# First block of a fused kernel: weight remainders one step later, gates by tanh, modulation through landing halves, bias remainder on VectorE

## The reference, cut to what matters

```python
mod = silu(c) @ w_ada + b_ada             # 1024 x 6144: twelve slabs of 512 columns, ada0 to ada11
h, hc = norm(x) * (1 + sc) + sh, norm(ctx) * (1 + sc_c) + sh_c      # slabs 0 to 3
na_k, na_v, ml_k, ml_v, ml_g, na_q, ml_q, ml_o, gate_na, gate_ml = split(h @ w_in)   # ctx: the first five
o_na = neighbourhood_attention(...)       # 8 heads of 64, 256 queries, 256 + 256 keys
o_ml = mlstm(...)                         # 4 heads, both directions
merged = sigmoid(gate_na) * (o_na @ w_branch_na) + sigmoid(gate_ml) * (o_ml @ w_branch_ml)
x = x + gt_m * rmsnorm(merged @ w_out, g_mix_post)
x = x + gt_f * rmsnorm(moe_ffn(...))      # 32 experts, 12.6 MB of weights each
x = second_block(x)                       # two layers
```

## Time and profile before

| | |
|---|---|
| median of 3 runs | 2408.9 us (2406.7 to 2418.7) |
| the profiled execution | 2409.3 us, its span 2407.5 us |
| first block up to the first expert matmul | 0 to 440 us of the span |
| experts | 440 to some 1360 us |
| second block | to 2407.5 us |
| TensorE busy, mean granted clock | 91%, 0.971 |

### The profile page before, as it was taken

How to read it: one execution, slowest core, us unless ns; L and a number is a source line. 1 busy time by engine, 2 the same in 40 slices (tenths; PEclk the granted TensorE clock), 3 DMA queues, 4 the chain that set the end, 5 groups by cost and what they waited for, 6 DMA issues and landing times.

```text
span 2407.5 us, 33072 instructions
## 1 busy us (share of the span) xinstructions
PE 2201.5 (91%) x13860; PEld 1569.3 (65%) x13860; DVE 929.6 (39%) x1355; ACT 734.7 (31%) x969; POOL 28.1 (1%) x32
## 2 busy tenths in 40 slices
PE   5999888999889888988998899999999799999998
PEld 4887676433333333333333488998999698998997
DVE  4456575311111121111121265366344454474453
ACT  4124552211101111111111245444433444544432
POOL 0000011000000000000000000000000000000000
PEclk8999998999999999999999999999999899999998
DMA  9462156699999999999999934544444454443542
GB/s 359 165 225 90 53 158 212 255 428 427 427 427 428 428 427 428 427 428 428 426 428 428 358 113 159 160 163 153 145 162 167 141 168 148 147 170 137 178 154 92
DMA packets 139388, 626.98 MB, mean 260 GB/s; under 512 B 7703, under 2 KB 33831, under 8 KB 114407
## 3 DMA queue, kind: packets, MB, share of 16 engines
q1 hardware_dynamic: 131808, 609.87, 65.0%
q0 software_dynamic: 5184, 13.90, 2.0%
q10 hardware_dynamic: 2247, 1.01, 0.2%
HBM read 623.69 MB, written 1.05 MB: 259 GB/s over the span
## 4 chain that ended last, share of the span: by engine, by line
PE 65%; DMA 23%; DVE 5%; issue 3%; ACT 3%; SPq 1%; ACTq 0%; DVEq 0%; POOL 0%
DMA ring<-in_w_lin 20%; PE bank L1598 15%; PE bank L1687 12%; PE bank L1922 10%; PE bank L1937 5%; PE bank L1845 3%; DMA ring<-in_w_in 2%; PE bank L1268 2%; PE bank L1316 2%; PE bank L1864 1%; DVE ring_rounded L2027 1%; PE bank L1711 1%; PE bank L1253 1%; PE bank L1696 1%; PE bank L1465 1%
## 5 line engine op out<-in xcount | busy, mean ns | idle before, releaser
L1598 PE MATMUL bank<-ring,arenaA 128*64 128x512 f32 x3072 | 692.9, 601 | 39.3 <-DMA ring<-in_w_lin 28.6
L1598 PEld LDWEIGHTS bank<-ring,arenaA 128*64 128x64 f32 x3072 | 211.0, 138 | 462.1 <-issue 390.3
L2475 DVE TENSOR_TENSOR ring_rounded<-ring,ring_rounded 128x2048 fp32r<-128x2048 f32 (+1 forms) x160 | 338.1, 2152 | 148.1 <-ACT ring_rounded L964 148.1
L964 ACT ACTIVATE ring_rounded<-ring 128x2048 fp32r<-128x2048 f32 (+1 forms) x160 | 280.4, 1799 | 284.7 <-DMA ring<-in_w_in 116.2
L1687 PE MATMUL bank<-arena_rounded,ring_rounded 128*128 128x256 f32 x2496 | 308.9, 284 | 0.0
L1687 PEld LDWEIGHTS bank<-arena_rounded,ring_rounded 128*128 128x128 f32 x2496 | 301.1, 190 | 4.1 <-issue 3.1
L1922 PE MATMUL bank<-arena_rounded,ring_rounded 128*128 128x256 f32 x2112 | 256.0, 282 | 1.2 <-DVE arena_rounded L2665 1.0
L1922 PEld LDWEIGHTS bank<-arena_rounded,ring_rounded 128*128 128x128 f32 x2112 | 252.8, 190 | 4.6 <-ACT arena_rounded L1106 3.0
L2421 DVE TENSOR_SCALAR arenaA<-bank 128x512 f32<-128x512 f32 x32 | 22.1, 692 | 502.4 <-PE bank L1598 502.4
L945 ACT ACTIVATE arenaA<-bank 128x512 f32<-128x512 f32 x32 | 19.1, 597 | 328.8 <-PE bank L1643 328.8
L1937 PE MATMUL bank<-arena_rounded,ring_rounded 128*128 128x256 f32 x912 | 110.0, 283 | 2.3 <-DVE arenaA L2677 2.3
(11 more groups left out here) (385 smaller groups left out, 2210.6 us busy)
## 6 DMA issues: line engine op xcount, KB each, us to landing
ring<-in_w_gate SPq DMA_DIRECT2D x64, 2048.0 KB, 23.3
ring<-in_w_lin SPq DMA_DIRECT2D x64, 2048.0 KB, 25.6
ring<-in_w_down SPq DMA_DIRECT2D x64, 2048.0 KB, 21.8
ring<-in_w_in SPq DMA_DIRECT2D x34, 2048.0 KB, 12.0
ring<-in_w_ffn_gate SPq DMA_DIRECT2D x10, 2048.0 KB, 8.1
ring<-in_w_ffn_up SPq DMA_DIRECT2D x10, 2048.0 KB, 7.8
ring<-in_w_ffn_down SPq DMA_DIRECT2D x12, 1536.0 KB, 6.4
ring<-in_w_in SPq DMA_DIRECT2D x16, 1024.0 KB, 8.0
```

The source lines that it names most:

```text
L964: act.activation(place2(name + "_hi", ringR)[:, a:b, :], place2(name)[:, a:b, :], ACT.Copy).then_inc(w_hi, 1)
L1598: last = pe.matmul(bank[b][k * SLOTS:(k + 1) * SLOTS, :], lhsT(c), slot(j)[:, c % 4, k * 512:(k + 1) * 512], start=False, stop=(c == DC - ...
L2475: dve.tensor_tensor(place2(name, ringR)[:, a:b, :], w[:, a:b, :], hi[:, a:b, :], ALU.subtract).then_inc(w_lo, 1)
```

## The change

- nak0 and nak1 become one 2 MB slab nak, with its high part in place 5; the rounding has two pieces, each ahead of one of the copies of ada rows 2 and 3.
- ada10 and ada11 leave the ring. All slabs 4 to 11 come through the landing buffers; each buffer has a semaphore and is refilled as soon as its own four steps are done. The folds 4 to 11 all stand in the projections, and so do VectorE's steps for them. The load of the gate columns (mlgRaw) is issued behind ada4 on GpSimd's queue.
- The ring is filled up with two empty slabs, so expert 0's first loads go to places 4, 5 and then 0 to 3.
- Attention: ScalarE rounds gate h+2 in the even step, VectorE forms its remainder in the odd one; bna0 and bna1 follow in the last two heads; the later remainders move up by one.
- Gates: tanh(x/2) in place of sigmoid(x); the branch product is multiplied by (1 + gate), which doubles merged; scale 0.5 in the output's squares and in gpost takes it out.
- out1 is rounded right behind the square root of the head norm.
- The bias remainder is formed by VectorE behind out3's remainder; ScalarE's copy for it moves behind the rounding of out3.
- Eight identity matmuls on TensorE behind the turns of ada2 and ada3.

```diff
-        adaRow = [Pna[:, 1, :] if i < 4 else wide(AT_MLO, 2, 512, arenaA)[:, i % 2, :] if i < 10 else cossin[:, :]
-                  for i in range(12)]
+        adaRow = [Pna[:, 1, :] if i < 4 else wide(AT_MLO, 2, 512, arenaA)[:, i % 2, :] for i in range(12)]
...
-        slabs += [(f"nak{i}", half(C_NAK + 256 * i)) for i in range(2)]
-        slabs += [("nav", w_in[:, :, C_NAV:C_MLK]), ("nav_hi", None),
+        slabs += [("nak", w_in[:, :, C_NAK:C_NAV]), ("nak_hi", None), ("nav", w_in[:, :, C_NAV:C_MLK]), ("nav_hi", None),
...
-        for k in range(8):
-            slabs += [(f"gate{k}", half(gate_at[k]))]
-            if k in (0, 2):
-                slabs += [(f"ada{10 + k // 2}", ada_src(10 + k // 2))]
+        slabs += [(f"gate{k}", half(gate_at[k])) for k in range(8)]
...
+        slabs += [(None, None)] * (-len(slabs) % RING)
...
+        ORDER1 = [f"na_k{m}" for m in range(4)] + ["na_v0", "na_v1", "ada4", "na_v2", "ada5", "na_v3", "ml_k0", "ada6", "ml_k1", "ada7",
+                                                  "ml_v0", "ml_v1", "ml_v2", "ada8", "ml_v3", "ada9", "ml_g", "ml_q0", "ml_gt", "ada10",
+                                                  "na_q0", "ada11", "na_q1", "ml_o0", "ml_o1"]
...
-            for j in range(RING):
+            for j in (4, 5, 0, 1, 2, 3):
                 sp.wait_ge(*freed(N1 - RING + j))
                 expert_slab(0, j)
...
-            rounded1("nak0")
+            rounded1("nak", (0,))
             ada_copy(2)
-            rounded1("nak1")
+            rounded1("nak", (1,))
             ada_copy(3)
...
-                    empty(GATES[h], dst, ACT.Sigmoid, src=two)
-                    if h + 2 < 8:
-                        rounded1(f"gate{h + 2}")
-                    elif h == 7:
-                        rounded1("bna0")
+                    empty(GATES[h], dst, ACT.Tanh, scale=0.5, src=two)
+                elif h + 2 < 8:
+                    rounded1(f"gate{h + 2}")
+                elif h == 6:
+                    rounded1("bna0")
+                else:
+                    rounded1("bna1")
...
-                if dr == 1:
-                    rounded1(("bna1", "bml0", "bml1", "out0")[h])
+                if dr == 1 and h < 3:
+                    rounded1(("bml0", "bml1", "out0")[h])
...
             rounded1("out2")
             rounded1("out3")
+            act.wait_ge(bias_in, 16 * 6)
+            act.activation(bparts, braw, ACT.Copy).then_inc(bias_hi, 1)
             act.wait_ge(c_pos, 1)
...
+            for _ in range(8):
+                pe.matmul(bank[4][:, 0:P], K["ident"][:, :], K["ident"][:, :], start=True, stop=True)
...
-                pe.wait_ge(ada_sum, i - 3)
+                pe.wait_ge(ada_sum, 2 * (i - 3))
...
-                if i in (8, 14):
-                    ada_fold(9 + i // 7)
...
-                if i < 10:
-                    dve.wait_ge(ada_in, 32 * (i - 3))
-                    w = lambda c: adaX[c // 4][:, c % 4, :]
-                else:
-                    dve.wait_ge(*in1(f"ada{i}"))
-                    w = lambda c: raw1(f"ada{i}")[:, c, :]
+                w = lambda c: adaX[c // 4][:, c % 4, :]
                 for c in chunks:
+                    if c % 4 == 0:
+                        dve.wait_ge(ada_in[c // 4], 16 * (i - 3))
...
             rest1("nav")
             ada_part(4, range(8))
+            ada_part(5, range(4))
             rel_copy(0)
-            ada_part(5, range(4))
+            ada_part(5, range(4, 8))
+            rest1("mlk")
             rel_copy(1)
-            ada_part(5, range(4, 8))
+            modulation(4)
+            ada_part(6, range(8))
             rel_copy(2)
...
             rest1("naq0")
             rest1("naq1")
-            modulation(6)
-            ada_part(8, range(8))
-            modulation(7)
+            modulation(8)
+            ada_part(10, range(8))
+            modulation(9)
+            ada_part(11, range(4))
...
-                if qt and h + 2 < 8:
-                    rest1(f"gate{h + 2}")
+                if qt:
+                    rest1(f"gate{h + 2}" if h + 2 < 8 else f"bna{h - 6}")
...
-            rest1("bna0")
...
-                link(dve.tensor_tensor(gm, bank[g % 4][:, :].rearrange("p (a b) -> p a b", a=2), gm, ALU.mult))
+                link(dve.scalar_tensor_tensor(out=gm, in0=gm, scalar=1.0, in1=two(bank[g % 4][:, :]), op0=ALU.add, op1=ALU.mult))
...
             rest1("out2")
             rest1("out3")
+            dve.wait_ge(bias_hi, 1)
+            for k in range(2):
+                r = slice(64 * k + 32, 64 * k + 64)
+                dve.tensor_tensor(bparts[r, :, :], braw[r, :, :], bparts[r, :, :].bitcast(F32), ALU.subtract).then_inc(bias_lo, 1)
...
-            pool.dma_start(mlgRaw, w_in[:, :, C_MLG:C_NAQ]).then_inc(bg_in, 16)
-            for i in range(4, 10):
-                pool.wait_ge(*((lin_done, G1["ada3"] + 1) if i == 4 else (ada_sum, i - 4)))
+            pool.wait_ge(lin_done, G1["ada3"] + 1)
+            for i in range(4, 12):
                 for k in range(2):
-                    pool.dma_start(adaX[k], ada_src(i)[:, 4 * k:4 * k + 4, :]).then_inc(ada_in, 16)
+                    if i > 4:
+                        pool.wait_ge(ada_sum, 2 * (i - 5) + k + 1)
+                    pool.dma_start(adaX[k], ada_src(i)[:, 4 * k:4 * k + 4, :]).then_inc(ada_in[k], 16)
+                if i == 4:
+                    pool.dma_start(mlgRaw, w_in[:, :, C_MLG:C_NAQ]).then_inc(bg_in, 16)
...
-            pool.wait_ge(bias_hi, 1)
-            for k in range(2):
-                r = slice(64 * k + 32, 64 * k + 64)
-                pool.tensor_tensor(bparts[r, :, :], braw[r, :, :], bparts[r, :, :].bitcast(F32), ALU.subtract).then_inc(bias_lo, 1)
```

107 lines of the change are left out of this document (48 added, 59 removed).

## The result

The changed kernel takes 2391.5 us (median of 4 runs, 2388.2 to 2396.2), the kernel before 2408.9; the ratio is 0.9928, with a 95% interval of 0.9903 to 0.9954, 17.4 us between the medians. The forecast was 2392.3 us and -17.0.

A forecast was written before the change was run, and what follows sets the result against it. TensorE and what it waits for bound the first 440 us; the experts' weight stream behind, at 427 GB/s, only moves with it. Terms summed to -17.0 us, from 2409.3 to 2392.3 us; range 2384 to 2402.

The forecast's parts named there:

- Attention, -17.8: Attention stage: without late loads and waits TensorE alone sets the pace, 11.15 us a pair; 17.8 us shorter, bounds -14 and -18.3.
- Projections: folds +1.9: Projections: the two folds moved here from the attention take 0.95 us each, adding 1.9 us.
- Fold 11, +1.1: End of projections: fold 11 waits 3.2 us where fold 9 waited 2.09, adding 1.1 us; bounds -1.3 and +5.2.
- No further half-speed groups: Projections: no more groups of 24 matmuls than before take 7.38 instead of 5.83 us at the dropped clock.
- Rival 1: Projections: folds behind more short rel matmuls bring three more clock drops, +4.7 us, 2397 us; chance 0.14.
- Start, +1.7: Start: both roundings and row copies come behind the whole nak slab's landing, adding 1.7 us; bounds +0.4 and +2.4.
- mLSTM and branches, -1.1: mLSTM: no table load ahead of the first weights, -0.8 us; no out0 remainder ahead of the head norm, -0.3 us.
- Output, -2.9: Output product: VectorE's angle chain ends at 388.1 instead of 391.0 us, saving 2.9 us; bounds -6 and +2.8.
- Rival 3: Projections: the modulation stream becomes the bound; at landings of 16 us +33 us, 2425 us, slower than before; chance 0.04.
- Rival 5: Experts: the gain doesn't arrive because their weight stream starts no sooner, 2409 us; chance 0.03.

## Why the prediction came out right, and where it did not

*Attention, -17.8.* Right in mechanism and size (-18.6). Its parts, by the runs: the ring 14.5 us, the roundings' place 6.3, together 20.8 from a kernel at 112.7, where the one before took 110.5; tanh nothing. The view that TensorE alone would bound the stage, at 11.15 us a pair, held (11.07), and so did the 0.7 for the last copy.

*Projections: folds +1.9* holds. *Fold 11, +1.1*: wrong in size and sign. The last half landed in 5.7 us, not 7.8, and the wait was 0.80 us, not 3.2; -1.3 was the lower bound that I had named. The step at fault is that landing, which I put near the median of before, 8.5 us; that median takes in the ring's slabs, and GpSimd's own loads had 7.7 there and 5.8 in the changed kernel. Why they land sooner isn't shown; the DMA queues still moved 354 GB/s in those 5.7 us. Undoing the halves shows that the mechanism is right: 4.63 us.

*No further half-speed groups.* This step failed: two more in both traces of the changed kernel, +3.1 us. Rival 1 (three more, +4.7) was the nearer story in its number, and the groups at 78 and 127 us, which I took as evidence against it, are two that now have a drop. Its cause is not shown: the first of the two has no fold ahead of it, and the same order of work had five or four slow groups in four other traces. At four, the stretch of 89.2 us is that of before (87.45) and two folds. There is one trace of before, so whether it has six in other executions, and whether the 3.1 us are the change's at all, stays open. The low clock also sat elsewhere: the gate logs' sums take 1.7 us more and the rotated products 1.8 less; these cancel.

*Start, +1.7* (measured +2.0): the order of roundings and copies is the cause, as costed; the runs add that it was avoidable.

*mLSTM and branches, -1.1*: as measured. *Output, -2.9*: the idle fell by 2.7; the stage gained 3.5, because the matmuls of b_ml ahead of it took 13.15 us for 13.98.

*Rival 3* (the stream of modulation slabs as bound) never came near: folds 4 to 10 waited for nothing, even with the landing place whole. *Rival 5*: the stream starts 17.5 us sooner, and 17.2 of it arrive behind the experts. That VectorE work could hold up the last landing by 0.5 us, for which the prediction cited the Trainium skill, is not seen in its 5.7 us.

The sum of -17.0 against -17.5 is closer than its terms, and that is luck: +3.0 that was missing in the projections, -2.5 at fold 11, -0.8 in the attention and -0.7 at the output nearly cancel.

## What to carry to other kernels

When an engine waits for a copy, look at what stands ahead of the copy in its queue, and at what the load behind that waits for: here that was a ring place which only a later fold on TensorE freed, and it was the largest term. Order each queue by who is waited for: two copies of 0.6 us behind a landing cost some 4.5 us, a signal at the end of a chain rather than at the one value that was needed cost 5. And allow, in the price of a wait of TensorE, for a low clock behind it: here 1.4 to 4.8 us behind a wait of 2.54. Last, before a difference of a few microseconds is put down to an edit, take out the stretches that the edit doesn't touch.

## What the runs showed of the hardware

- A wait of 2.54 us was followed by 13.04 us of matmuls that take 8.2 at full clock. The same wait before was followed by a head_out of 3.33 us, 1.4 too much, and in the kernel with ring and roundings put back by a head_out of 3.12 and scores of 2.45 us, 1.6 too much: what followed one wait differs threefold.
- Matmuls of 63x48 (f32) and 128x512 (rounded operands) in turn took 0.77 us a pair at full clock, in blocks of one kind 0.48.
- Groups of 24 matmuls behind short ones ran at the low clock four, five or six times in traces with the same order of work, 89.2 to 92.4 us.
- The same second block, some 7658 matmuls, took 1014.1 to 1023.8 us.
- At the start the same matmuls ran at either level of the clock in different executions: the products with the fourth modulation slab ended at 39.1 or at 44.0 us. While nak's landing at 42.1 set the start, this hardly showed; with nak in halves it is worth 3.7 us.
